# Gate and up tiles of the third feed-forward stage as seven half products in place of eight

## What is computed

```python
h = h + 0.5 * swiglu(rmsnorm(h, norm_ffn1[0]), ...)        # feed-forward 0
h = h + ab_mixer(rmsnorm(h, norm_mix[0]), ...)
h = h + 0.5 * swiglu(rmsnorm(h, norm_ffn2[0]), ...)        # feed-forward 1
gate = sigmoid(rmsnorm(h, norm_ple[0]) @ w_ple_gate[0])
h = h + gate * (p[0] @ w_ple_proj[0])                      # "ple" stage 0
h = h + 0.5 * swiglu(rmsnorm(h, norm_ffn1[1]), ...)        # feed-forward 2, the one changed
h = h + c_mixer(rmsnorm(h, norm_mix[1]), ...)
...
def swiglu(x, w_gate, w_up, w_down):
    return (silu(x @ w_gate) * (x @ w_up)) @ w_down        # 1024 -> 2816 -> 1024
```

## Time and profile before

| | us |
|---|---|
| median of 3 executions | 3317.61 |
| the profiled execution | 3314.88 |
| its span in the trace | 3313.6 |
| PE busy in the span | 3213.5 (97%) |
| DVE busy | 1528.2 (46%) |
| ACT busy | 1067.6 (32%) |
| POOL busy | 308.9 (9%) |

### The profile page before, as it was taken

The page is one execution under the profiler, slowest core; times in us unless marked ns, Lnnn a source line. Parts: engine busy times, 40 slices in busy tenths (PEclk is TensorE's granted clock), DMA queues, the critical chain, the costliest instruction groups (busy, mean ns, idle before and its releaser), DMA issues. The chain is left out here.

```text
span 3313.6 us, 46922 instructions
## 1 busy us (share of the span) xinstructions
PE 3213.5 (97%) x20296; PEld 2465.6 (74%) x20296; DVE 1528.2 (46%) x2218; ACT 1067.6 (32%) x1594; POOL 308.9 (9%) x365
## 2 busy tenths in 40 slices
PE   9999999999999999999999999979999999989988
PEld 7888887888888888889788888768877888424332
DVE  5443456644435544332754434685567544301112
ACT  4222226432223322322632223553344323200001
POOL 1000131200001000000210001211111301100000
...
GB/s 145 102 90 90 145 145 40 39 102 89 90 97 109 100 95 90 96 107 109 84 89 102 98 88 91 113 20 50 3 65 20 105 99 126 337 427 425 425 427 345
DMA packets 62798, 448.77 MB, mean 135 GB/s; under 512 B 8704, under 2 KB 10368, under 8 KB 32640
## 3 DMA queue, kind: packets, MB, share of 16 engines
...
...
## 5 line engine op out<-in xcount | busy, mean ns | idle before, releaser
L568 DVE TENSOR_TENSOR w_lo<-slot,w_hi 128x2048 fp32r<-128x2048 f32 (+4 forms) x243 | 487.3, 2005 | 331.5 <-ACT w_hi L559 329.3
L167 PE MATMUL bank<-xa,w_hi 128*128 128x512 f32 x1368 | 535.7, 392 | 2.0 <-DVE w_lo L3162 2.0
L168 PE MATMUL bank<-xa,w_hi 128*128 128x512 f32 x1368 | 532.4, 389 | 0.0
L169 PE MATMUL bank<-xa,w_lo 128*128 128x512 f32 x1368 | 532.3, 389 | 0.0
L559 ACT ACTIVATE w_hi<-slot 128x2048 fp32r<-128x2048 f32 (+4 forms) x243 | 406.1, 1671 | 335.5 <-PE bank L169 327.0
L167 PE MATMUL bank<-xb,w_hi 128*128 128x512 f32 x832 | 324.7, 390 | 0.8 <-DVE w_lo L568 0.7
L169 PE MATMUL bank<-xb,w_lo 128*128 128x512 f32 x832 | 323.7, 389 | 0.0
L168 PE MATMUL bank<-xb,w_hi 128*128 128x512 f32 x832 | 323.7, 389 | 0.0
L167 PEld LDWEIGHTS bank<-xa,w_hi 128*128 128x128 f32 x1368 | 256.7, 188 | 63.1 <-issue 5.4
L168 PEld LDWEIGHTS bank<-xa,w_hi 128*128 128x128 f32 x1368 | 256.8, 188 | 53.9 <-issue 1.2
L169 PEld LDWEIGHTS bank<-xa,w_lo 128*128 128x128 f32 x1368 | 256.8, 188 | 53.7
...
## 6 DMA issues: line engine op xcount, KB each, us to landing
slot<-in_w_gu SPq DMA_DIRECT2D x87, 1024.0 KB, 4.8
...
```

The lines of the kernel that those rows point to most:

```text
L167: e.matmul(out, w[0], x[0], start=(j == 0), stop=False)
L168: e.matmul(out, w[0], x[1], start=False, stop=False)
L169: return e.matmul(out, w[1], x[0], start=False, stop=(j == n - 1))
L568: dve.e.tensor_tensor(lo, slot(k, b), hi.bitcast(F32), ALU.subtract).then_inc(L.up("w_lo", b))
```

## The change

The weights of a step are taken as a 2x2 matrix of blocks: gate and up by the first and second half of the contraction (512 each). The input is a 2x2 matrix too: first and second half of the contraction by first and second half of the tokens (256 each). Before, that was eight block products. Now it is seven, by a Strassen-like scheme: each multiplies a sum of weight blocks by a sum or difference of input blocks, and the four output quarters are sums of the seven results. A product is 4 tiles x 3 = 12 matmuls of 256 columns, a step 84.

- The sums of weight blocks are made by three means. HBM holds a copy of the weights in which blocks are repeated (4096 columns a step in place of 2048). SP brings 3072 columns of it (`sp_raw`, two DMAs, three buffers `raw7`). POOL issues two accumulating DMAs a step (`pool_comb`): 1024 columns from HBM added to two blocks, then one of these blocks added to the pair block. DVE makes the last sum (`dve_comb_sum`).
- For each product ACT rounds its weight block (`act_comb`) and DVE makes the remainder (`dve_comb`), into a ring of eight places.
- The combinations of the input are made in the ple stage (`act_seven_x`, `dve_seven_x`), in place of the gained half of `act_norm` and of `dve_norm` for this norm. On DVE a tile i < 4 takes three instructions 256 wide (`x5_diff`, `x1_lo`, and `x5_lo`, which waits for ACT's `x5_hi`), a tile from 4 on takes five, as the diff shows.
- DVE puts the quarters together (`dve_seven`: `gate_left`, `two_more`, `rest`, `up_right`, `ends`), ACT helps with one copy (`first_part`). Only the gate is scaled by `rstd`, and the down product is scaled afterwards, in an instruction of its own.
- The rounded and remainder parts of `hid` lie where inputs and weight buffers lay. They are made in the last step (0 to 9) and after it (10 to 21), no longer step by step.

The diff, cut to its core:

```diff
+SEVEN_ORDER = (1, 5, 2, 6, 7, 3, 4)
...
+SEVEN_READY = {1: "x1_lo", 5: "x5_lo", 2: "x23_lo", 3: "x23_lo", 6: "x674_lo", 7: "x674_lo", 4: "x674_lo"}
...
+def seven_free(k, f, s):
+
+    if s < 8:
+        return ("w_used", k.first[f"gu{f}"] - (2 if s < 4 else 1))
+    return ("seven", f, s - 8 if s < 152 else s - 4)
...
+        pe.wait_ge(*L.at("comb_lo", f, s))
+        for j in range(4):
+            c, t = slice(SEVEN_X[p] * 256, SEVEN_X[p] * 256 + 256), slice(j * P, (j + 1) * P)
+            x_lo, x_hi = cols(k.sv.x[j][:2], c)
+            pe.wait_ge(*L.at(SEVEN_READY[p], nm, j))
+            e.matmul(out, hi[:, t], x_hi, start=(j == 0), stop=False)
+            e.matmul(out, hi[:, t], x_lo, start=False, stop=False)
+            last = e.matmul(out, lo[:, t], x_hi, start=False, stop=(j == 3))
+        last.then_inc(L.up("seven", f, s))
+
+    for m in range(FF):
+        for p in SEVEN_ORDER:
+            product(p, m)
+            if m == 0 and p == 6:
+                pe_norm(k, nm)
...
+def dve_seven_x(k, nm, i):
...
+    else:
+        dve.wait_ge(*L.at("x2_f32", nm, j))
+        e.tensor_tensor(low[:, 1280:1536], low[:, 768:1024], high[:, 1280:1536], ALU.subtract).then_inc(L.up("x7_diff", nm, j))
+        dve.wait_ge(*L.at("x7_diff", nm, j))
...
+        dve.wait_ge(*L.at("x6_diff", nm, j))
...
+        dve.wait_ge(*L.at("x23_hi", nm, j))
+        dve.wait_ge(*L.at("x4_diff", nm, j))
+        e.tensor_tensor(lo[:, 512:1024], low[:, 512:1024], top[:, 512:1024], ALU.subtract).then_inc(L.up("x23_lo", nm, j))
+        dve.wait_ge(*L.at("x674_hi", nm, j))
+        e.tensor_tensor(lo[:, 1024:1792], low[:, 1024:1792], top[:, 1024:1792], ALU.subtract).then_inc(L.up("x674_lo", nm, j))
...
+def pool_comb(k, f, m):
+
+    pool, L, b = k.pool, k.led, k.first[f"gu{f}"] + m
+    pool.wait_ge(*L.at("w_in", b))
+    pool.e.dma_start(k.sv.raw[m % 3][:, 1536:2560], k.order[b][0][:, 3072:4096], accum_op=ALU.add).then_inc(
+        L.up(f"raw_sum{m % 3}", b, by=16, also=[("w_sum", b)]), 16)
+    pool.wait_ge(*L.at("w_sum", b))
+    pool.e.dma_start(k.sv.pairs[m % 3], seven_raw(k, 5, m), accum_op=ALU.add).then_inc(
+        L.up(f"raw_sum{m % 3}", f"{b}", by=16, also=[("w_sum2", b)]), 16)
...
+def act_seven(k, f, nm):
...
+    for m in range(FF):
+        more = m + 1 < FF
+        if more:
+            act_comb(k, f, 1, m + 1)
...
+        e.activation(sv.first, k.banks.of("one", f, m)[:, 0:256], ACT.Copy).then_inc(L.up("first_part", f, m))
+        if more:
+            act_comb(k, f, 5, m + 1)
+        if m:
+            silu(m - 1)
+        if m == 0:
+            act_root(k, nm, k.rstd_last)
+        if more:
+            for p in (2, 6, 7, 3, 4):
+                act_comb(k, f, p, m + 1)
...
+    dve_weight(k, d0 + 1)
+    for j in range(10, FF):
+        dve_hid_lo(k, f, j)
...
+        if layer == 0 and i == KT - 1:
+            for p in (1, 5, 2, 6):
+                dve_comb(k, SEVEN_FFN, p, 0)
...
-            dve_norm(k, nx, i, gain, k.xa)
+            dve_seven_x(k, nx, i)
...
-    pool_norm(k, "n4")
+    for m in range(FF):
+        if m == 2:
+            pool_norm(k, "n4")
+        pool_comb(k, SEVEN_FFN, m)
```

More of the change, by code:

```diff
@@ L44 @@
 SIGNALS = {kind: sem for sem, kinds in {
+    "mixer_sums": "ple_gate ple_proj gate2 pool_mix branch rot qk_sum qk_spread seven",
+    "mixer_curves": "class_hi v_out p_hi edge_hi raw_in qk_sq qk_root yr_hi gate2_sigmoid mg_hi h_scaled",
+    "mixer_vectors": "ple_scaled ple_gated qk_part qk_scaled qk_inv qk_scale root_part root_sum gate2_scaled branch_gated merge_add mg_lo yr_lo p_lo",
+    "seven_curves": "comb_hi first_part x_f32 x1_hi x5_hi x2_f32 x23_hi x674_hi",
+    "seven_vectors": "comb_lo comb_sum gate_left two_more rest up_right ends gate_ready hid_full x5_diff x1_lo x5_lo x7_diff x6_diff x4_diff x23_lo x674_lo",
     "rwkv_sums": "kk_sum kk_spread low ysum bonus_sum ysq_sum y_spread g_sum",
@@ L235, in __init__, with plan_seven, area, block @@
         self.rb = [rb[:, i * P:(i + 1) * P] for i in range(3)] if rb is not None else [a.buf(P, "den_inv") for _ in range(3)]
+def plan_seven(k):
+    m, made = Kernel(), []
+    def area(start, size):
+        a = Arena(k.nc, start, made)
+        a.end = start + size
+        return a
+    def block(a):
+        b = a.copy()
+        return (a.buf(7 * 256, "xc_lo", F32R), a.buf(7 * 256, "xc_hi", F32R), b.buf(7 * 256, "x_low"), b.buf(7 * 256, "x_high"))
+    def pair(a):
+        b = a.copy()
+        return (a.buf(512, "comb_hi", F32R), a.buf(512, "comb_lo", F32R), b.buf(512, "comb_full"), b.buf(512, "comb_full"))[:4]
+    slots, parts, x, z = 3432, 11624, 19816, 28008
+    a = area(x, 8192)
+    m.x = [block(a), block(a)]
+    m.pairs = [a.buf(512, "raw7") for _ in range(2)] + [area(2880, 512).buf(512, "raw7")]
+    a = area(z, 12800)
+    b = a.copy()
+    hid_lo, m.hidden = [a.buf(512, "hid7_lo", F32R) for _ in range(FF)], [b.buf(512, "hidden") for _ in range(FF)]
+    m.four = a.buf(1024, "four")
+    m.first, m.two = a.buf(256, "first_part"), a.buf(256, "two_part")
+    a = area(z + 12800, 7168)
+    hid_late = [a.copy()]
+    m.x += [block(a), block(a)]
+    b = hid_late[0]
+    late = [b.buf(512, "hid7_hi", F32R) for _ in range(12)]
+    assert b.at <= a.at
+    m.raw = [a.buf(5 * 512, "raw7") for _ in range(2)]
+    b = area(a.at - 5120, 5120)
+    early = [b.buf(512, "hid7_hi", F32R) for _ in range(10)]
+    m.hid = [(hi, lo) for hi, lo in zip(early[5:] + early[:5] + late, hid_lo)]
+    a = area(slots + 1536, 2560)
+    m.raw += [a.buf(5 * 512, "raw7")]
+    a = area(parts, 8192)
+    m.ring = [pair(a) for _ in range(8)]
+    return m
 def plan_memory(k):
@@ L486, in plan_weights @@
     k.slot_of, k.part_of = {}, {}
+    gu, dn = k.first[f"gu{SEVEN_FFN}"], k.first[f"dn{SEVEN_FFN}"]
+    k.raw_of = {}
     for b, (src, n, split) in enumerate(k.order):
+        if gu <= b < dn:
+            m = b - gu
+            k.raw_of[b] = (m % 3, ("comb_lo", SEVEN_FFN, seven_turn(4, m - 3)) if m > 2 else ("w_lo", gu - 1) if m == 2 else ("down", 1, 7))
+            continue
+        if b == dn:
+            assert slots[0] == parts[0] == 0
+            held[1] = ("comb_lo", SEVEN_FFN, seven_turn(4, FF - 2))
+            part_held = {0: ("seven", SEVEN_FFN, 147), 1: ("seven", SEVEN_FFN, 153)}
         if b == k.first["g2_pool"]:
@@ L645, in pe_idle, with seven_raw @@
     last.then_inc(L.up("idle", name))
+SEVEN_ORDER = (1, 5, 2, 6, 7, 3, 4)
+SEVEN_BANK = {1: "one", 5: "mid", 2: "two", 6: "six", 7: "mid", 3: "end", 4: "end"}
+SEVEN_FREE = {"one": "first_part", "mid": "up_right", "two": "gate_left", "six": "two_more", "end": "ends"}
+SEVEN_X = {1: 0, 5: 1, 2: 2, 3: 3, 6: 4, 7: 5, 4: 6}
+SEVEN_READY = {1: "x1_lo", 5: "x5_lo", 2: "x23_lo", 3: "x23_lo", 6: "x674_lo", 7: "x674_lo", 4: "x674_lo"}
+SEVEN_RAW = {1: 0, 2: 512, 4: 1024, 7: 1536, 5: 2048}
+def seven_raw(k, p, m):
+    return k.sv.pairs[m % 3] if p == 6 else k.sv.raw[m % 3][:, SEVEN_RAW[p]:SEVEN_RAW[p] + 512]
@@ L650, in pe_ffn @@
     x, hid, b0, d0 = k.ffn_x[f], k.ffn_hid[f], k.first[f"gu{f}"], k.first[f"dn{f}"]
-    for m in range(FF):
+    if f == SEVEN_FFN:
+        pe_seven(k, f, nm)
+    for m in range(FF) if f != SEVEN_FFN else ():
         w = views(part(k, b0 + m), "p (g k c) -> p g k c", g=2, k=KT)
```

229 lines of the change are left out of this document (219 added, 10 removed).

## The result

The changed kernel takes 3342.24 us, the median of 4 executions (3339.21 to 3343.81), where the kernel before took 3318.45 beside it (3317.11 to 3320.07). The ratio is 1.007, with an interval of 1.0053 to 1.0088: slower by 24 us, where 5 us faster was forecast, and outside the range. Its profiled span is 3342.5 us, 28.9 more than before. First the windows, with the same columns as the earlier trace rows: the ple stage with PE's wait behind it, the start of the changed stage up to the end of product 6, the rest of the stage, and the wait ahead of the down product.

A forecast was written before the change was run, and what follows sets the result against it. PE was taken to bound the gate and up steps. Matmuls -22.7, hand-over +12.9, root and reciprocal +2.0 and end +3.0 summed to -4.8 us, from 3317.6 to 3312.8 us; range 3303 to 3326.

The forecast's parts named there:

- matmuls, 22 steps: Gate and up steps on PE: 84 matmuls at 0.1173 us make 9.85 a step against 10.88, saving 22.7 us.
- hand-over, to the end of product 6: From ple stage into step 0: late adds to h and PE's wait for the last tile's x23_lo cost 12.9 us.
- end of the stage: Behind PE's last product: DVE finishes the step late, PE waits for hid_lo of tile 10; 2.3 to 3.5, taken as 3.0 us.
- The price of an addition: POOL's 512 KB adding DMA: taken as 5 us, between 3.1 and 9.6, costing nought in the steps; above 8 setting the pace.
- a rival at 3335: Rival on POOL: additions take 9 us or more, its step 10.5 to 11, ple sums 10 us later; 3335 us, chance 0.08.
- the chain of one buffer: Weights in the steps: load and two additions on one buffer, 6 + 5 + 4 us, covered by two steps, some 20 us.
- two serial additions hold POOL to 1056: Hand-over: additions issued ahead of n4's sums keep POOL until about 1056, where its first sum had started at 1049.20.
- The hand-over's chain on DVE: DVE's cycle per tile in the ple stage: 6.4 us for tiles 1 to 3, 8.35 for tiles 4 and 5.
- DVE in a step: Fifteen DVE instructions a step sum to 9.5 to 9.7 us, covered by PE's 9.85; cost nought.
- Root and reciprocal: Right after the hand-over: remainders of step 1 queue behind DVE's and ACT's root and reciprocal, delaying PE; cost 2.0 us.
- Rival (1): Hand-over costs half, 6.4 us, with POOL free before 1055; 3306.4 us, chance 0.20.
- Rival (4): Matmuls of 256 columns take 109 ns, but DVE's 9.6 us a step limits the gain to 5.3; 3307.5 us, chance 0.04.

The follow-up runs named there:

- e1: The changed kernel without POOL's two adding DMAs a step and the waits for them; 3319.77 us, ratio 1.0007.
- e2: The changed kernel with POOL's two DMAs a step overwriting instead of adding, same sizes, places and waits; 3321.18 us.
- e4: The changed kernel with SP's load split, the 512 KB that is added to first, and the first addition waiting for that alone; 3326.03 us.
- e6: e3 and e4 together, plus own places for the last step's products 3 and 4 and earlier down weights; 3314.51 us.
- e12: e6 with step 0's remainders moved behind the add to h[7], plus two unread 512-wide DVE instructions in steps 1 to 17; 3327.49 us.
- e3: The changed kernel with POOL's sum of squares 1 ahead of its first addition and later issues between the sums; 3340.43 us.
- e10: e6 with DVE and ACT reordered behind the last product and step 0's remainders in DVE's waits around h[6] and h[7]; 3311.78 us.

## Why the prediction was wrong

The terms of its sum, against the profiles of the changed kernel, of e1 (no additions) and of e2 (copies, at the price that I had taken for additions). "Steps, over the matmuls" is the time from the end of product 6 to the last product, less 150 x 12 x 0.120 = 216.0 and the 0.9 of the norm's matmul that was there before. The last term is the time from the end of the last product to the start of the last down matmul, less the 119.5 of before.

| term | predicted | changed kernel | e1 | e2 |
|---|---|---|---|---|
| matmuls, 22 steps | -22.7 | -17.6 | -17.6 | -17.6 |
| hand-over, to the end of product 6 | +12.9 | +22.0 | +12.4 | +14.7 |
| steps, over the matmuls | +2.0 | +13.8 | +1.7 | +1.7 |
| end of the stage | +3.0 | +7.9 | +7.5 | +7.5 |
| sum | -4.8 | +26.1 | +4.0 | +6.3 |

The hand-over is 1111.92 - (1083.83 + 48 x 0.120) = 22.3 less the 0.26 of before. These are times from the start of the span, and the changed kernel reaches the norm's matmul in the ple stage (1033.79 before) 0.5 us later, e1 0.9 and e2 0.3 later; so much of each hand-over lies ahead of it. The spans differ by 28.9, the medians by 23.8; the other 2.8 of the span lie behind the stage, where nothing was changed, and are not explained.

- **The price of an addition** is the step that failed most: "I take 5, nearer the row of equal size". It was 8.4, and 9.2 in the steps, within my bounds of 3.1 and 9.6, and I had written that above 8 it would set the pace. POOL's step was indeed 10.98, and "cost nought" became the 13.8 of the table. I then gave this case a chance of 0.08, as a rival at 3335, with the mechanism right in both places. The bounds of an operation that no row shows should have set that chance. What the price broke in the steps is the chain of one buffer, which I had put at 6 + 5 + 4 = 15 us: the load landed after 8.6, the additions after 9.2 and 5.4, together 23 where two steps of PE have 20.2. e4 bears this out: with additions of 8.6 that begin behind the first 512 KB, POOL's step is 9.8 and PE waits for nothing in the steps. That two serial additions hold POOL to 1056 failed with the price: 1063.7, and the later adds to h came 7.7 to 7.9 us late. By e2 some 1.8 of that are not the adding but the first raw block, which landed at 1045 to 1046 where I had 1042. About 1.4 more at the hand-over are 15 matmuls at the lower clock (0.53 from 1108.7 to 1111.9), which I had put in the range only.
- **The matmuls** failed by a count. 0.1173 rested on 191 starts, and 0.120 was set aside as that of "the nine before them", where the nine were 192. That is 5.1 us.
- **The end** failed because I did not ask what a place of the ring in the last step waits for. The condition stands in the diff in front of the prediction, `s - 4`. DVE waited 4.6 us there in e1. PE then did not wait where I had said, at tile 10, but 4.4 us at once for the first down weights and 1.2 later on; 3.0 became 7.5. In e6, with places of their own and earlier down weights, the term is 4.2.
- **The hand-over's chain on DVE** was right in its cycles: 6.4 and 8.35 us came out as 6.46 and 8.34. That in e1 the six adds h[2] to h[7] stand within 1.0 us of the working, and the whole term at 12.4 for 12.9, is in part luck: the working has h[2] 1.5 us late for POOL, which e1 does not have, and e1 came 0.9 late to the stage. At the price that I had taken the term is e2's 14.7.
- **DVE in a step** was right as a cover: 9.44 us measured, 9.5 to 9.7 predicted, and it does not set the pace. e12 shows from where on it would. Its margin of 0.64 does more than I said: it pays back, over nine or ten steps (e1, e4), what DVE is late at the start.
- **Root and reciprocal** cost 1.7 in e1 where 2.0 was said: PE waited 0.4 for a remainder, as predicted, and then 0.8 for DVE to free a bank, which the working did not have.
- **Rival (1)**, that the hand-over costs half, has nothing for it. Rival (4), 109 ns, has rows at 0.120 against it everywhere.

Had the price of the addition alone been right, the time would have been near e2's 3321.2: no gain either. Without any additions (e1) the scheme saves 17.6 us of matmuls in this stage and pays 12.4 at the hand-over, 1.7 in the first steps and 7.5 at the end; only with the additions fitted in and the seams reworked (e3 to e10) is it 5.8 us faster than the kernel before.
